# Rotary partner of q and k: from reordered weight copies to permutation matmuls on chip

## The chip, the cores and the metric

The kernel runs on the 8 cores of one Trainium2 chip. Each core takes one of the 8 sequences and runs the same program; nothing passes between the cores. The time is the device time in microseconds of the slowest core, in one launch.

## The reference, cut to what matters

One layer of a streaming encoder over 8192 prompt tokens and 64 sample tokens per core, width 1024: a SwiGLU feed-forward (hidden width 2816) with a LayerNorm, one input projection, sliding-window attention beside a gated recurrence (RG-LRU), an output projection with a LayerNorm, a second feed-forward with a LayerNorm, and a gated embedding. What the change touches is the rotation of q and k behind the input projection:

```python
z = h @ w_in            # [q 512 | k 128 | v 128 | x_lru 512 | gate_lru 512]
def _rope(x, pos):      # x: heads of 64; only the first 16 of each head turn
    x1, x2 = x[..., :8], x[..., 8:16]
    return concat([x1*cos - x2*sin, x2*cos + x1*sin, x[..., 16:]])
q = _rope(q, pos); k = _rope(k, pos)
```

So every turned element needs itself times cos plus its partner (eight columns away in its head) times plus or minus sin.

## The kernel before

**Tiles.** The prompt is cut into 16 tiles of 512 tokens and one last tile of 64 sample tokens, worked one after the other by `tile_prog`. A tile has four subtiles of 128 tokens. `hbuf` holds them token by token in f32; `to_feature_major_s` (lines 655 to 667) turns a subtile with TensorE transposes (L359) into `actT` (bf16, features on the partitions), which ScalarE (q=0) and VectorE (q=1) copy out of PSUM.

**Weights.** No weight stays on the chip. They stream through a ring of `NS` = 6 slots of 1 MB, block by block (`BLOCKS`, lines 159 to 183), 48 blocks to a tile: 11 `up` blocks, 6 `dn` blocks (two halves `hf`, three parts `g` each), 6 `in` blocks (in0 the columns of q, in1 those columns once more with the partners exchanged, in2 the k columns in four versions: plain, partners exchanged, heads exchanged, both; in3 the recurrence, in4 the gate, in5 v), 4 output blocks (`oa`, `ol`), 17 for the second feed-forward, 4 at the end. `w_acquire` names the slot, `w_release` frees it and calls `w_pump` (line 548), which issues the load of the block six places on (an `up` block of both weights is one block). The ring loads are on the SP queue (SyncE), in block order, and SP waits at each until its slot is free.

**Preparation.** The weights arrive in f32 with another layout. In the first tile only, `w_pump` calls `prep_block` (lines 408 to 485) ahead of each block's first load: DMAs on the POOL queue (GpSimd) that cast to bf16 and write `wstream` in device memory. The SP queue waits for a block's preparation before it loads it. These DMAs stand in POOL's program order among its other work, so what stands behind them on POOL (its part of `layer_norm`) is issued after them. Most blocks are 1 to 3 DMAs. in1 is 24 and in2 is 96 (lines 440 to 463), because the exchange of 8 columns by 8 is done by small DMAs, for each of the 8 slices of 128 rows. in0, in1 and in2 are pumped when the three `dn` blocks of half 0 are released, in3, in4 and in5 when those of half 1 are.

**The first feed-forward's end.** In half 1, as each subtile s is done, VectorE adds it to `hbuf`, TensorE turns subtile s-2, and `layer_norm(s)` follows: VectorE (statistics, `nb`), POOL (`rstd`), ScalarE (scale and shift), VectorE (times gamma), POOL (plus beta, 128x1024, L370 `hbuf<-hbuf,bbc`). The turns of subtiles 2 and 3 are left in `pending_T`, for `flush_T`.

**Input projection, where the change is (lines 717 to 762).** Tokens 0 to 255 are worked first, then `flush_T`, then tokens 256 to 511. For each half and each of four 128-column chunks `qc` of q, `inproj_chunk` runs 8 matmuls (256 tokens wide) from in0 into one PSUM bank and 8 from in1 into another. VectorE multiplies the first by `rope_c` into `ftA` and the second by `rope_s` into `ftB`; POOL adds them into `qT`. `ftA` and `ftB` have two buffers each. Then k: two variants (`var`), each two chunks of 8 matmuls of 512 tokens from in2, two multiplications and one POOL add into `kT`. Then v: 32 matmuls of 128 columns from in5, copied by ScalarE. Then the mixed stage, in which steps of attention and of the recurrence alternate; its first matmuls (`attn_A(0)`) read `qT` and `kT`.

**Order and waits.** Every engine runs its instructions in program order. `Prog` turns named reads and writes into semaphore waits. Banks go round eight (`bank`).

**Setup.** SP loads constants. POOL clears `wbd_f`, SP loads 16 small blocks of the recurrence's weights into it, POOL casts it to `wbd`, and then POOL's first preparation DMA is issued.

Of the kernel before, what the change touches and what calls it, by code (L numbers as in the profile page):

```python
# [28 lines left out]
NBLK = 48  # L29
# [129 lines left out]
def block_table():  # L159
# [9 lines left out]
    for i in range(6):  # L169
        blocks.append(("in", i))  # L170
# [19 lines left out]
def blk_extent(b):  # L190
# [6 lines left out]
    if k == "in":  # L197
        return (128, 4096) if b[1] < 5 else (128, 1024)
# [11 lines left out]
def build(ntiles_prompt=SEQ // TILE, with_sample=True):  # L210
# [36 lines left out]
    ident_d = din("ident", [128, 128])  # L247

# [35 lines left out]
    ident = sb("ident_sb", [128, 128])  # L284
    ones_b = sb("ones_b", [128, 64], BF16)
# [8 lines left out]
    wbd_f = sb("wbd_f", [128, 2, 4, 128])  # L294
# [113 lines left out]
    def prep_block(bi):  # L408
# [17 lines left out]
        elif k == "in":  # L426
            j = b[1]
            src = win_d.rearrange("(k p) c -> p k c", p=128)
            if j < 5:
                o4 = dst.rearrange("p (k c) -> p k c", k=8)  # L430
# [6 lines left out]
            elif j == 5:  # L437
                o = dst[:, 0:1024].rearrange("p (k c) -> p k c", k=8)
                prep(o, src[:, :, 640:768])
            elif j == 1:  # L440
                for kk in range(8):
                    o5 = o4[:, kk, :].rearrange("p (h d) -> p h d", h=8)
                    s5 = src[:, kk, 0:512].rearrange("p (h d) -> p h d", h=8)
                    prep(o5[:, :, 16:64], s5[:, :, 16:64])
                    prep(o5[:, :, 0:8], s5[:, :, 8:16])
                    prep(o5[:, :, 8:16], s5[:, :, 0:8])
            elif j == 2:
                for kk in range(8):
                    kcols = src[:, kk, 512:640]
                    prep(o4[:, kk, 0:128], kcols)  # L450
                    o5 = o4[:, kk, 128:256].rearrange("p (h d) -> p h d", h=2)
                    s5 = kcols.rearrange("p (h d) -> p h d", h=2)
                    prep(o5[:, :, 16:64], s5[:, :, 16:64])
                    prep(o5[:, :, 0:8], s5[:, :, 8:16])
                    prep(o5[:, :, 8:16], s5[:, :, 0:8])
                    prep(o4[:, kk, 256:320], kcols[:, 64:128])
                    prep(o4[:, kk, 320:384], kcols[:, 0:64])
                    for hh in range(2):
                        od = o4[:, kk, 384 + hh * 64:384 + (hh + 1) * 64]
                        sd = kcols[:, (1 - hh) * 64:(2 - hh) * 64]  # L460
                        prep(od[:, 16:64], sd[:, 16:64])
                        prep(od[:, 0:8], sd[:, 8:16])
                        prep(od[:, 8:16], sd[:, 0:8])
# [31 lines left out]
    sdma(ident[:], ident_d)  # L495
    for i in range(3):
# [8 lines left out]
    mset("pool", wbd_f[:], 0.0, ("wbdf_ms",))  # L505
    P.final_sems.add("setup2")
    wn = 0
    for ax, src in enumerate((wa_d, wx_d)):
        for cc in range(4):
            for hh in range(2):  # L510
                wn += 1
                o_ = dma("sp", wbd_f[hh * 64:(hh + 1) * 64, ax, cc, hh * 64:(hh + 1) * 64], src[cc * 2 + hh],
                         ("wbdf_ms",), ("wbdf_%d" % wn,), "setup2", nonc=True)
                P.last_w["wbdf"] = o_
    cp("pool", wbd[:], wbd_f[:], ("wbdf", "wbdf_ms"), ("consts2",))
# [157 lines left out]
    def tile_prog(ti, seq, tok0, T, pos0, first, last, nxt=None, preloaded=False):  # L673
# [43 lines left out]
        def inproj_chunk(blk, ci, t0=0, t1=None):  # L717
# [4 lines left out]
            for k in range(8):  # L722
                mm(psum[bk][:, 0:t1 - t0], rg[:, k * 512 + ci * 128:k * 512 + (ci + 1) * 128], actT[:, k, t0:t1],
# [4 lines left out]
        ri = 0  # L728
        for hi_, (t0, t1) in enumerate(halves):
            if hi_ == len(halves) - 1:  # L730
                flush_T()
            W_ = t1 - t0
            for qc in range(4):
                bq = inproj_chunk(0, qc, t0, t1)
                bs = inproj_chunk(1, qc, t0, t1)
                fa, fb = ftA[ri % 2], ftB[ri % 2]
# [380 lines left out]
```

How the kernel before makes its waits and increments, by code:

```python
            def body(eng):  # L134
                for o in prog.streams[engname]:
                    for key, d, fin in o.waits:
                        if key[0] == "d":
                            v = prog.dma_cnt[d.dsem] if fin else d.dval
                            eng.wait_ge(dsems[d.dsem], v)
                        else:
                            eng.wait_ge(esem[d.eng], d.cnt)
                    ins = o.fn(eng)
                    if o.dsem is not None:
                        ins.then_inc(dsems[o.dsem], 16)
                    elif o.signal:
                        ins.then_inc(esem[engname], 1)
                if engname == "sp":
                    for k, v in prog.dma_cnt.items():
                        eng.wait_ge(dsems[k], v)
```

## Time and profile before

| | us |
|---|---|
| median of 2 runs | 7746.52 |
| the two runs | 7599.89 and 7893.15 |
| the profiled execution's own time | 7616.16 |
| its span, slowest core (core 3) | 7614.6 |
| its fastest core (core 0) | 7536.8 |
| TensorE busy | 6090.4 (80%) |
| VectorE, ScalarE, GpSimd busy | 3036.2, 1632.1, 1044.4 |

The span runs from the first to the last instruction. The busy time of TensorE counts matmuls that are waiting in its pipeline, so 80% is not 80% of its peak. "Granted clock" is the share of TensorE's full clock (2.4 GHz) that it was given; its lower level is one half (1.2 GHz). All times in the rows are of core 3.

### The profile page before, as it was taken

The page shows a single profiled execution, that of the slowest core. Times are in us where ns is not written, and L with a number is a line of the kernel's source. Part 1 is how long each engine was busy: PE and PEld are TensorE (multiplying, and loading weights), DVE is VectorE, ACT ScalarE, POOL GpSimd, SP SyncE. Part 2 cuts the span into 40 slices and gives each one's busy share as a digit, 9 for nine tenths or more (in the row PEclk, how much of TensorE's full clock was granted, in tenths as well). Part 3 has the DMA queues.
Part 4 walks back from the last instruction along what each step waited for, and adds up shares of the span by engine and source line. Part 5 has one row for each costly group of instructions (what it writes and reads, how often), then busy time and mean ns, then how long its engine had stood idle before and what let it go on. Part 6 is the DMA issues. An engine that isn't in the chain of part 4 may idle for free.

```text
span 7614.6 us, 100795 instructions; the slowest of 8 cores (7536.8 to 7614.6 us)
## 1 busy us (share of the span) xinstructions
PE 6090.4 (80%) x33302; PEld 3325.1 (44%) x33302; DVE 3036.2 (40%) x5649; ACT 1632.1 (21%) x3079; POOL 1044.4 (14%) x1329
## 2 busy tenths in 40 slices
PE   4226698888888898888888888888888888888884
PEld 2113254444444454444444444444454454444442
DVE  1013244343434444443434434443444444353432
ACT  0012122131312122131312112131212113131211
POOL 1132011110201111110201110110201111010110
PEclk9657798989898998989898998989898898989886
DMA  9997823424242332424242332424232342424336
GB/s 159 75 59 104 172 96 112 144 93 143 74 155 77 136 126 107 150 84 152 74 151 80 129 133 102 154 78 154 78 140 91 116 146 95 150 84 149 82 134 200
DMA packets 272280, 901.92 MB, mean 118 GB/s; under 512 B 72896, under 2 KB 145920, under 8 KB 191264
## 3 DMA queue, kind: packets, MB, share of 16 engines
q1 hardware_dynamic: 154864, 818.91, 31.5%
q0 software_dynamic: 116912, 76.56, 19.9%
q8 instruction: 282, 4.62, 0.3%
q14 instruction: 222, 1.82, 0.1%
HBM read 906.19 MB, written 78.92 MB: 129 GB/s over the span
## 4 chain that ended last, share of the span: by engine, by line
PE 56%; issue 13%; DVE 10%; ACT 8%; DMA 6%; POOL 4%; another core or an unknown queue 2%; SPq 0%; DVEq 0%; ACTq 0%; POOLq 0%
PE ps_all L356 54%; DVE stats L640 3%; ACT hbuf L367 2%; DMA hbuf<-x 2%; DVE hbuf L378 2%; PE ps_all L359 2%; DVE L_xc L378 1%; DMA ring<-wstream 1%; POOL wstream L400 1%; POOL rstd L370 1%; DMA y<-hbuf 1%; ACT LS L367 1%; ACT PT L367 1%; ACT LA L367 1%
## 5 line engine op out<-in xcount | busy, mean ns | idle before, releaser
L356 PE MATMUL ps_all<-actT,ring 128*128 128x512 bf16 (+2 forms) x18784 | 3301.1, 340 | 276.5 <-DMA ring<-wstream 122.6
L356 PEld LDWEIGHTS ps_all<-actT,ring 128*128 128x128 bf16 x18784 | 1839.9, 103 | 1655.5 <-issue 451.1
L356 PE MATMUL ps_all<-ring,hid 128*128 128x512 bf16 (+1 forms) x5720 | 1270.9, 384 | 118.1 <-DMA ring<-wstream 117.4
L378 DVE SCALAR_TENSOR_TENSOR ftB<-ftA,ps_all 128x512 f32<-128x512 f32 (+2 forms) x1070 | 612.3, 572 | 1569.3 <-ACT ftA L367 1471.7
L367 ACT ACTIVATE ftA<-ps_all 128x512 f32<-128x512 f32 (+2 forms) x1070 | 539.3, 505 | 2355.9 <-PE ps_all L356 2012.7
L356 PEld LDWEIGHTS ps_all<-ring,hid 128*128 128x128 bf16 (+1 forms) x5720 | 564.7, 99 | 806.0 <-issue 155.0
L359 PE MATMUL ps_all<-ident_sb,hbuf 128*128 128x128 f32 (+1 forms) x2080 | 310.8, 306 | 569.4 <-POOL hbuf L370 274.9
L367 ACT ACTIVATE hbuf<-hbuf,nb,rstd 128x1024 f32<-128x1024 f32 (+1 forms) x195 | 241.8, 1240 | 2278.0 <-DVE nb L378 2278.0
L378 DVE SCALAR_TENSOR_TENSOR hbuf<-hbuf,ps_all 128x512 f32<-128x512 f32 (+1 forms) x390 | 267.0, 685 | 929.6 <-PE ps_all L356 929.6
L370 DVE TENSOR_TENSOR hid<-ftB,ps_all 128x512 bf16<-128x512 f32 (+2 forms) x940 | 523.7, 557 | 175.6 <-PE ps_all L356 102.8
L374 POOL TENSOR_SCALAR rstd<-mv 128x1 f32<-128x1 f32 (+1 forms) x195 | 43.2, 222 | 3766.4 <-DVE mv L642 3766.3
L359 PEld LDWEIGHTS ps_all<-ident_sb,hbuf 128*128 128x128 f32 (+1 forms) x2080 | 269.1, 160 | 635.3 <-issue 634.3
L370 POOL TENSOR_TENSOR hbuf<-hbuf,bbc 128x1024 f32<-128x1024 f32 (+1 forms) x195 | 458.5, 2351 | 612.6 <-DVE hbuf L370 605.8
L356 PE MATMUL ps_all<-Vb,PT 128*64 128x65 bf16 (+1 forms) x2048 | 373.2, 244 | 122.3 <-ACT PT L367 89.2
L356 PEld LDWEIGHTS ps_all<-Vb,PT 128*64 128x64 bf16 (+1 forms) x2048 | 242.3, 119 | 270.4 <-issue 163.2
L370 DVE TENSOR_TENSOR hbuf<-hbuf,gbc 128x1024 f32<-128x1024 f32 (+1 forms) x195 | 238.8, 1225 | 293.5 <-ACT hbuf L367 293.5
L356 PE MATMUL ps_all<-ring,actT 128*128 128x512 bf16 (+2 forms) x1560 | 309.0, 350 | 29.9 <-DMA ring<-wstream 26.9
L640 DVE BATCH_NORM_STATS2 stats<-hbuf 128x6 f32<-128x512 f32 (+1 forms) x390 | 269.5, 691 | 31.4 <-DVE stats L640 0.9
L383 DVE CAST actT<-ps_all 128x512 bf16<-128x512 f32 x260 | 175.2, 682 | 258.0 <-PE ps_all L359 255.7
L382 ACT CAST actT<-ps_all 128x512 bf16<-128x512 f32 x260 | 149.4, 575 | 389.4 <-PE ps_all L359 389.3
L356 PEld LDWEIGHTS ps_all<-ring,actT 128*128 128x128 bf16 (+1 forms) x1560 | 140.7, 104 | 171.2 <-issue 69.4
L367 ACT ACTIVATE PT<-ps_all 64x256 bf16<-64x256 f32 (+1 forms) x512 | 194.6, 380 | 43.0 <-PE ps_all L356 16.3
(94 smaller groups left out, 3159.9 us busy)
## 6 DMA issues: line engine op xcount, KB each, us to landing
ring<-wstream SPq DMA_DIRECT2D x629, 1024.0 KB, 5.9
ring<-wstream SPq DMA_DIRECT2D x68, 768.0 KB
ring<-wstream SPq DMA_DIRECT2D x68, 512.0 KB, 4.6
y<-hbuf SPq DMA_DIRECT2D x64, 512.0 KB, 5.2
hbuf<-x POOLq DMA_DIRECT2D x60, 512.0 KB, 10.4
ring<-wstream SPq DMA_DIRECT2D x51, 256.0 KB, 3.0
wstream<-ffn_wg POOLq DMA_DIRECT2D x22, 512.0 KB, 48.8
wstream<-ffn_wu POOLq DMA_DIRECT2D x22, 512.0 KB, 58.5
```

The lines of the kernel that those rows point to most:

```text
L356: return P.op("pe", lambda e: e.matmul(out, lhsT, rhs, start=start, stop=stop), reads, writes)
L359: return P.op("pe", lambda e: e.transpose(out, in_, idn), reads, writes)
L367: return P.op("act", lambda e: e.activation(out, in_, func, **kw), reads, writes)
L370: return P.op(eng, lambda e: e.tensor_tensor(out, a, b, op), reads, writes)
L374: return P.op(eng, lambda e: e.tensor_scalar(out, a, s1, None, op0), reads, writes)
L378: return P.op("dve", lambda e: e.scalar_tensor_tensor(out, a, s, b, op0, op1), reads, writes)
L382: return P.op("act", lambda e: e.copy(out, in_), reads, writes)
L383: return P.op(eng, lambda e: e.tensor_copy(out, in_), reads, writes)
L400: return e.dma_start(out=out, in_=in_)
L640: P.op("dve", lambda e, c=c: e.bn_stats(stats[0:nt, c, :], hv[0:nt, c * 512:(c + 1) * 512]), (hn,), (sn,))
```

## The change

It drops block in1 and three of the four versions in block in2: 47 blocks to a tile, in2 is 256 KB instead of 1 MB. The partner values come from a matmul with a constant 0/1 matrix: ScalarE copies the q chunk out of PSUM into a bf16 buffer `qb`, and one matmul with `perm[:, 0, :]` as weights gives its rows exchanged. Each q item is finished one item late (`pend`), so that the next chunk's 8 matmuls stand between the copy and the permutation. For k there is one chunk of 8 matmuls, one copy and three permutation matmuls (partners, heads, both); nothing stands between copy and permutations. In setup the three matrices are loaded by SP and cast by VectorE, and `wbd` is built in two passes through `ftB`, one after the other.

```diff
-    for i in range(6):
+    for i in (0, 2, 3, 4, 5):
         blocks.append(("in", i))
...
-            elif j == 1:
-                for kk in range(8):
-                    o5 = o4[:, kk, :].rearrange("p (h d) -> p h d", h=8)
-                    s5 = src[:, kk, 0:512].rearrange("p (h d) -> p h d", h=8)
-                    prep(o5[:, :, 16:64], s5[:, :, 16:64])
-                    prep(o5[:, :, 0:8], s5[:, :, 8:16])
-                    prep(o5[:, :, 8:16], s5[:, :, 0:8])
             elif j == 2:
-                for kk in range(8):
-                    kcols = src[:, kk, 512:640]
-                    prep(o4[:, kk, 0:128], kcols)
...
+                o = dst[:, 0:1024].rearrange("p (k c) -> p k c", k=8)
+                prep(o, src[:, :, 512:640])
...
+    perm_f = ftA[0][:, 0:384].rearrange("p (a b) -> p a b", a=3)
+    dma("sp", perm_f, perm_d, (), ("ftA0",), "permld")
+    cp("dve", perm[:], perm_f, ("ftA0",), ("consts2",))
...
-    mset("pool", wbd_f[:], 0.0, ("wbdf_ms",))
     for ax, src in enumerate((wa_d, wx_d)):
+        stage = ftB[ax][:, :].rearrange("p (c d) -> p c d", c=4)
+        mset("pool", ftB[ax][:, :], 0.0, ("ftB%d" % ax,))
         for cc in range(4):
             for hh in range(2):
...
+        cp("pool", wbd[:, ax, :, :], stage, ("wbdf%d" % ax, "ftB%d" % ax), ("consts2", "ftB%d" % ax))
-    cp("pool", wbd[:], wbd_f[:], ("wbdf", "wbdf_ms"), ("consts2",))
...
+        items = [(hi_, t0, t1, qc) for hi_, (t0, t1) in enumerate(halves) for qc in range(4)]
+        pend = []
+        def q_finish(it, bq, ri):
+            hi_, t0, t1, qc = it
+            W_ = t1 - t0
+            bs = bank()
+            mm(psum[bs][:, 0:W_], perm[:, 0, :], qb[ri % 2][:, 0:W_], True, True, ("qb%d" % (ri % 2),) + CONST,
+               ("ps%d" % bs,))
+            fa, fb = ftA[ri % 2], ftB[ri % 2]
+            tt("dve", fa[:, 0:W_], psum[bq][:, 0:W_], rope_c[:, t0:t1], ALU.mult,
+               ("ps%d" % bq, "rope"), ("ftA%d" % (ri % 2),))
+            tt("dve", fb[:, 0:W_], psum[bs][:, 0:W_], rope_s[:, t0:t1], ALU.mult,
+               ("ps%d" % bs, "rope"), ("ftB%d" % (ri % 2),))
+            tt("pool", qT[:, qc, t0:t1], fa[:, 0:W_], fb[:, 0:W_], ALU.add,
+               ("ftA%d" % (ri % 2), "ftB%d" % (ri % 2)), ("qT",))
+        for ri, it in enumerate(items):
+            hi_, t0, t1, qc = it
+            if hi_ == len(halves) - 1 and qc == 0:
+                flush_T()
+            bq = inproj_chunk(0, qc, t0, t1)
+            cp("act", qb[ri % 2][:, 0:t1 - t0], psum[bq][:, 0:t1 - t0], ("ps%d" % bq,), ("qb%d" % (ri % 2),))
+            if pend:
+                q_finish(*pend.pop())
+            pend.append((it, bq, ri))
+        q_finish(*pend.pop())
...
-        for var in range(2):
-            bq = inproj_chunk(2, var * 2)
-            bs = inproj_chunk(2, var * 2 + 1)
+        bkk = inproj_chunk(2, 0)
+        cp("act", qb[0][:, 0:T], psum[bkk][:, 0:T], ("ps%d" % bkk,), ("qb0",))
+        bks, bkd, bkds = bank(), bank(), bank()
+        for pi_, bb in ((0, bks), (1, bkd), (2, bkds)):
+            mm(psum[bb][:, 0:T], perm[:, pi_, :], qb[0][:, 0:T], True, True, ("qb0",) + CONST, ("ps%d" % bb,))
+        for var, (bq, bs) in enumerate(((bkk, bks), (bkd, bkds))):
```

## Rows read from the trace of the kernel before

**Rows 1.** Cores: span and mean granted clock of the slowest.

```profile
core 3: 7614.6 us, clock 0.859
```

**Rows 2.** Waits, 0 to 960 us: engine, line, releaser; total us, times, longest.

```profile
PE ps_all L356 <- DMA ring<-wstream: 259.0, 33, 48.7
PE ps_all L359 <- POOL hbuf L370: 152.9, 2, 149.0
```

**Rows 3.** Timeline of TensorE in the first tile: start, length, ..., idle before.

```profile
263.79 3.57 PE L356 MATMUL ps_all<-ring,hid 128*128 128x512 bf16 x8 [11.16 <-DMA ring<-wstream]
316.06 12.28 PE L356 MATMUL ps_all<-ring,hid 128*128 128x512 bf16 x50 [48.70 <-DMA ring<-wstream]
477.34 1.94 PE L359 MATMUL ps_all<-ident_sb,hbuf 128*128 128x128 f32 x8 [149.00 <-POOL hbuf L370]
...
547.67 3.46 PE L356 MATMUL ps_all<-ring,actT 128*128 128x128 bf16 x32 [26.94 <-DMA ring<-wstream]
```

**Rows 4.** Timeline of GpSimd in the first tile.

```profile
348.90 28.99 POOL L400 DMA_DIRECT2D wstream<-w_in  x47 [72.65 <-issue]
...
495.71 2.36 POOL L370 TENSOR_TENSOR hbuf<-hbuf,bbc 128x1024 f32<-128x1024 f32 x1 [3.13 <-DVE hbuf L370]
498.01 2.63 POOL L400 DMA_DIRECT2D wstream<-w_in  x3
```

**Rows 5.** Busy time by stretch: PE, PEld, DVE, ACT, POOL, granted clock, DMA share, GB/s.

```profile
200.00:250.00 50.00, 31.16 (x115) 12.20 (x114) 4.81 (x7) 1.19 (x2) 2.02 (x3) 0.80 1.02 158
...
350.00:400.00 50.00, 0.00 (x0) 0.00 (x0) 0.00 (x0) 0.00 (x0) 27.89 (x46) 0.50 7.24 9
```

**Rows 6.** DMA packets from 330 to 480 us.

```profile
DMA packets 28160, 3.60 MB, mean 24 GB/s; under 512 B 27904, under 2 KB 27904, under 8 KB 27904
```

**Rows 7.** DMA issues, whole span: out<-in, queue, count, KB each, us to landing.

```profile
wstream<-w_in POOLq DMA_DIRECT2D x32, 2.0 KB, 24.7
```

**Rows 8.** Ring loads issued on SP from 240 to 255 and from 255 to 270 us.

```profile
L352 SPq DMA_DIRECT2D ring<-wstream x1: 319/319/319, 249.6 to 249.6; - x1
L352 SPq DMA_DIRECT2D ring<-wstream x1: 320/320/320, 261.6 to 261.6; - x1
```

**Rows 9.** Timeline of TensorE in the second tile, around the input projection.

```profile
1072.86 8.48 PE L356 MATMUL ps_all<-actT,ring 128*128 128x256 bf16 x60 [0.94 <-DVE actT L383]
1081.18 1.91 PE L359 MATMUL ps_all<-ident_sb,hbuf 128*128 128x128 f32 x16
...
1084.82 13.62 PE L356 MATMUL ps_all<-actT,ring 128*128 128x256 bf16 x92 [0.64 <-DVE actT L383]
...
1101.02 0.51 PE L356 MATMUL ps_all<-qT,kT 64*128 64x128 bf16 x4 [0.80 <-POOL kT L370]
```

**Rows 10.** Timeline of GpSimd and of ScalarE there: the last LayerNorm.

```profile
1078.71 2.35 POOL L370 TENSOR_TENSOR hbuf<-hbuf,bbc 128x1024 f32<-128x1024 f32 x1 [3.12 <-DVE hbuf L370]
1076.00 1.24 ACT L367 ACTIVATE hbuf<-hbuf,nb,rstd 128x1024 f32<-128x1024 f32 x1 [5.33 <-DVE nb L378]
```

**Rows 11.** Groups by form: busy us, mean ns.

```profile
L382 ACT CAST actT<-ps_all 128x512 bf16<-128x512 f32 x256 | 147.9, 578 | 375.2 <-PE ps_all L359 375.2
...
L370 DVE TENSOR_TENSOR ftA<-ps_all,rope_c 128x256 f32<-128x256 f32 x128 | 54.0, 422 | 78.7 <-PE ps_all L356 42.1 <-POOL qT L370 34.4 <-DVE ftB L370 0.3
...
L382 ACT CAST pT<-ps_all 128x256 bf16<-128x256 f32 x64 | 23.5, 368 | 4.4 <-ACT pT L382 0.4
```

**Rows 12.** Timeline of the setup: SP's last 8 small loads, POOL's first preparation.

```profile
21.08 4.95 SPq L349 DMA_DIRECT2D wbd_f<-lru_wx  x8
...
29.65 1.14 POOL L400 DMA_DIRECT2D wstream<-ffn_wg  x1 [0.40 <-issue]
```

**Rows 13.** Busy time by stretch in the second tile, columns as in rows 5.

```profile
1070.00:1080.00 10.00, 8.15 (x54) 6.19 (x55) 6.63 (x12) 1.90 (x3) 4.43 (x4) 0.67 0.19 78
...
1140.00:1160.00 20.00, 15.27 (x91) 8.29 (x89) 10.93 (x28) 12.21 (x26) 1.61 (x4) 0.67 0.09 27
```

More of the change, by code:

```diff
@@ L28 @@
 SLOT = 4096
-NBLK = 48
+NBLK = 47
 HEAD_PERM = [0, 2, 1, 3, 4, 6, 5, 7]
@@ L247, in build @@
     ident_d = din("ident", [128, 128])
+    perm_d = din("perm", [128, 3, 128])
     y_d = dout("y", [NTOK, D])
@@ L284, in build @@
     ident = sb("ident_sb", [128, 128])
+    perm = sb("perm_b", [128, 3, 128], BF16)
+    qb = [sb("qb%d" % i, [128, TILE], BF16) for i in range(2)]
     ones_b = sb("ones_b", [128, 64], BF16)
@@ L727, in tile_prog @@
         halves = ((0, 256), (256, 512)) if T == TILE else ((0, T),)
-        ri = 0
-        for hi_, (t0, t1) in enumerate(halves):
-            if hi_ == len(halves) - 1:
-                flush_T()
[L732 to L736, printed above, removed]
-                tt("dve", fa[:, 0:W_], psum[bq][:, 0:W_], rope_c[:, t0:t1], ALU.mult,
-                   ("ps%d" % bq, "rope"), ("ftA%d" % (ri % 2),))
-                tt("dve", fb[:, 0:W_], psum[bs][:, 0:W_], rope_s[:, t0:t1], ALU.mult,
-                   ("ps%d" % bs, "rope"), ("ftB%d" % (ri % 2),))
-                tt("pool", qT[:, qc, t0:t1], fa[:, 0:W_], fb[:, 0:W_], ALU.add,
-                   ("ftA%d" % (ri % 2), "ftB%d" % (ri % 2)), ("qT",))
-                ri += 1
+        items = [(hi_, t0, t1, qc) for hi_, (t0, t1) in enumerate(halves) for qc in range(4)]
@@ L1066, in rope_tables, with perm_tables, partner @@
     return tab
+def perm_tables():
+    pm = np.zeros((128, 3, 128), np.float32)
+    def partner(d):
+        dd = d % 64
+        if dd < 8:
+            return d + 8
+        if dd < 16:
+            return d - 8
+        return None
+    for m in range(128):
+        p_ = partner(m)
+        if p_ is not None:
+            pm[p_, 0, m] = 1.0
+        sw = (m + 64) % 128
+        pm[sw, 1, m] = 1.0
+        p2 = partner(sw)
+        if p2 is not None:
+            pm[p2, 2, m] = 1.0
+    return pm
 _CACHE = {}
@@ L1084 @@
     ident = np.eye(128, dtype=np.float32)
+    perm = perm_tables()
     shared = {
@@ L1092 @@
         "lru_wx": f(lru_wx[0]), "lru_bx": f(lru_bx[0]), "lru_lambda": f(lru_lambda[0]),
-        "rope": rope, "ident": ident,
+        "rope": rope, "ident": ident, "perm": perm,
     }
```

30 lines of the change are left out of this document (8 added, 22 removed).

## The prediction

> **What bounds the kernel now.** I read the cores first: the slowest took 7614.6 us [rows 1]; its own time is 7616.16 us, 1.6 us more, and I count against that. It lies 1.7% below the median of the two runs and close to the lower one. Next come TensorE's longest waits in the first tile. It waited 259.0 us for ring loads and 152.9 us for one LayerNorm, 149.0 us of that in one piece [rows 2]. The timeline puts both in the first feed-forward's end [rows 3]. TensorE runs 8 matmuls at 263.79, then waits 48.70 us for the last `dn` load, runs 50 matmuls, and stands 149.00 us before the turn of subtile 0. The reader is to see what was late on the other side of each wait.
>
> On GpSimd the LayerNorm of subtile 0 stands behind the preparation of in1 and in2. POOL had waited 72.65 us when, at 348.90, it issued 47 small DMAs, and a second batch like it followed [rows 4]. In this time the DMA engines carried almost nothing: 158 GB/s at 200 to 250 us, 9 GB/s at 350 to 400, at a DMA share of 7.24, the sum of packets that overlap and all take long [rows 5]. Of 28,160 packets between 330 and 480 us, 27,904 were under 512 B [rows 6], from DMAs as small as 2 KB [rows 7]. The ring load of the last `dn` block was issued at 261.6 and its matmuls began at 316.06, 54.5 us later; the one before, issued at 249.6, began at 263.79, 14.2 us later [rows 3, 8]. So about 120 DMAs hold up both a ring load and a LayerNorm. That happens once, whatever the number of tiles.
>
> From the second tile on the input projection is bound otherwise. TensorE's first q half, 60 of its 64 matmuls in 8.48 us, and the turns of subtiles 2 and 3 at 1081.18 [rows 9] end where the last LayerNorm's POOL add ends, 1078.71 + 2.35 = 1081.06 [rows 10]. The second half, k and v run without a gap: 92 matmuls in 13.62 us. Attention then starts at 1101.02, with 0.80 us of waiting for `kT` [rows 9]. That stretch is TensorE's own.
>
> **Part 1: the small preparation goes (first tile).** 120 DMAs become one. The POOL queue then has in0, in2 and in3 ahead of the LayerNorm, all issued while other preparation drains. The last `dn` load would land 14.2 us after issue, at 275.8 instead of 316.06: 40.3 us. The 149.0 us wait goes except for the LayerNorm itself, which overlaps the 12.28 us of 50 matmuls; I leave 1 us of it, bounds 0 and 5: 148.0 us. Sum 188.3 us.
>
> What is late next: v. Its load waited for the preparation of in3, in4, in5, issued at 498.01 as the LayerNorm of subtile 3 ended [rows 4]; v began at 547.67, 49.7 us later, after 26.94 us of waiting [rows 3]. Now in3 is prepared earlier, one place ahead in the ring. Two preparations landed 12.0 us apart at 768 KB [rows 8], so 1 MB is 12 to 16 us; I take 14. v starts 14 us sooner against that LayerNorm. POOL issues eight `oa` DMAs ahead of the first q add in exchange (some 0.6 us each by the 28.99 us for 47 [rows 4], so 5 us), but v waits anyway: nothing. The q and k savings of this one tile are swallowed by the same wait. Sum for the first tile 188.3 + 14 = 202.
>
> in2 is still written in rows of 256 B, 1024 of them. 28,160 packets took these 150 us [rows 6], so 1024 take 5.5 us at the same rate; bounds 0 and 16 (as a 1 MB block). It is behind the `dn` blocks and TensorE wants it only for k, some 30 us later: nothing, up to 5.
>
> The Trainium skill bears on that (DMA: Bandwidth & Descriptors, Specifications): below 512 B a transfer becomes read-modify-write, so by it in2 stays on the slow side. The collapse to 9 GB/s with nearly all packets under 512 B agrees with it [rows 5, 6]. By the rule in2 costs as much per row as in1 did, and the sum would be up to 5 us less; by the wait for v, nothing.
>
> **Part 2: the matmuls (15 prompt tiles).** Per column the stretch of 92 matmuls gives 13.62 us / (60 x 256 + 32 x 512 = 31,744 columns) = 0.43 ns [rows 9].
> - First q half: half its matmuls go (32 x 256 columns, 3.5 us). But the turn of subtile 3 waits for the LayerNorm's add at 1081.06, which doesn't move. Also, the copies into `qb` stand on ScalarE behind the LayerNorm's activation, which ends at 1077.24 [rows 10], so the first permutation waits until about 1077.7, with chunks 2 and 3 queued behind it on TensorE. 0.9 + 0.9 us of chunks and three permutations fit before 1081. What is gained: VectorE's copies out of the turns come after three items instead of four, two operations of 0.42 us [rows 11]: 0.8 us.
> - Second q half and k: 64 x 256 + 32 x 512 = 32,768 columns become 32 x 256 + 8 x 512, plus 5 x 256 + 3 x 512 of permutations = 15,104. 17,664 x 0.43 = 7.6 us saved.
> - New waits: the last q permutation waits for its copy. A ScalarE copy of this size took 368 ns, one of 512 columns 578 ns [rows 11]; with 0.2 us of handing over, 0.6 us, and 0.8 us for k. Behind them stand TensorE's k chunk and v. The other copies are covered by the next chunk (8 x 256 columns, 0.9 us). VectorE needs 2 x 0.42 us to an item, under TensorE's 0.97: no new bound, but a thin one.
> - The k adds: `kT` is ready when two POOL adds are done, and v covers less of them; the wait of 0.80 us grows by some 0.6.
>
> Sum 7.6 + 0.8 - 0.6 - 0.8 - 0.6 = 6.4 us to a tile; 15 tiles: 96 us. Bounds: nothing (rival B) to the full column saving of both halves, 64 x 256 + 24 x 512 less 8 x 256 + 3 x 512 = 25,088 columns, 10.8 us; so 0 to 162 us in all.
>
> **Part 3: small ones.** Ring traffic falls by 1.75 MB a tile, but no wait of TensorE in the later tiles lies at in1 or in2: nothing. The sample tile has an eighth of the tokens: 6.4 / 8 = 0.8 us. Setup: the second eight small loads (4.95 us) now wait until the first eight landed and POOL has cast and cleared. That puts landing, cast and clearing, some 4 us, and the issue of `perm`'s load, 0.4 us, ahead of POOL's first preparation at 29.65 [rows 12]. All that follows in the first tile is paced by preparation, so it is paid: 4.4 us, bounds 0 and 8.
>
> **Sum.** 7616.2 - 202 - 96 - 0.8 + 4.4 = 7321.8: 7322 us, 3.9% less.
>
> **The rivals.**
> - B, the matmuls bring nothing. While TensorE waits for ScalarE in the first q half, its clock stays at the lower level: 0.67 was the mean at 1070 to 1080 [rows 13], and with still more holes there the rise comes later. If the second half and k run at 1.2 GHz, their 15,104 columns cost 6.5 us more, just what was gained. For it: three new places where TensorE stands. Against: from 1085 on work is dense. 7322 + 96 = 7418.
> - C, half of the first tile's stall stays: in0, in2 and in3 are now prepared in the same stretch, and ring loads share the DMA engines with them. For it: loads took up to 54.5 us there. Against: the load beside ordinary preparation took 14.2. 7322 + 100 = 7422.
> - D, TensorE saves in full, because the LayerNorm's end is no wall: 15 x (10.8 - 6.4) = 66 us more, 7256. Against: the first half ends within 0.2 us of that LayerNorm [rows 9, 10].
> - E, slower than before. The q, k and v stretch, broken by handovers, leaves TensorE on its lower level, and it enters the mixed stage so and stays. There 15.27 of 20 us are busy at a mean clock of 0.67 [rows 13]; at 0.5 the same work is 20.5 us, 5.2 more for each 20 us. For 80 us of mixed stage that is 21 us, with the 6.5 us of B 27, less the 6.4 gained: 21 us a tile, 315 us in all, 7616 - 202 + 315 = 7729. It decides from 14 us lost to a tile. Against: the stage has its own holes already and its clock is set by them.
> - F, the small DMAs' time was not the cause and the wait stays (the change doesn't do what it says): 7616 - 96 = 7520.
>
> The Trainium skill speaks for B and E (TensorE: Matmul & The Clock Gate, HAM oscillation): waits between bursts put the engine back on its half clock, and the warm-up is paid anew in each. No row here shows it for holes of 0.6 us.
>
> **How the numbers follow.** Forecast 0.56, B 0.17, C 0.11, D 0.09, E 0.03, F 0.04. A measurement tells about 2% from no change. The range goes from D's side, 7250, to beyond B and C, 7440. Faster by over 2% means below 7464: the forecast, B, C, D, in all 0.92 after leaving 0.01 of C out; within 2%: F and that 0.01, 0.05; slower 0.03.
>
> **What would show it.** Right: no TensorE wait over 30 us between 250 and 500 us; the turn of subtile 0 near 293 us (with the setup's 4.4); v near 350; the first tile some 200 us shorter; from `flush_T` to attention 6 us less a tile, and the turns of subtile 3 still ending with the POOL add. Wrong: a wait of 100 us left in front of a LayerNorm (F, C), a granted clock near 0.5 to 0.7 after `flush_T` (B), or in the mixed stage (E).

## The result, and the profile after

| us | before | after |
|---|---|---|
| median of the launches (10 and 11) | 7853.21 | 7405.99 |
| shortest launch | 7599.04 | 7317.11 |
| profiled execution, its own time | 7616.16 | 7366.27 |
| mean span of its 8 cores | 7577.5 | 7304.1 |

The ratio is 0.9638, 95% interval 0.9621 to 0.9655: 3.6% less time. The medians contain launches in which the cores of one die (four neighbouring cores) had a lower clock and took longer; the ratio leaves these out, and without them the launches took 7599 to 7600 us before and 7317 to 7334 us after, two of them 7322.

The rows of some cores in the profiled execution of after: cores 0 and 1 are the longest and have the lowest mean clock.

```profile
core 0: 7363.4 us, clock 0.854
core 1: 7336.4 us, clock 0.855
...
core 3: 7290.4 us, clock 0.856
...
core 5: 7277.0 us, clock 0.865
```

I read the first tile on core 3, as before, and the steady tiles on core 5. First the page's counts of after. Before, the page had 72,896 packets under 512 B of 272,280, and q0, the queue of the preparation, had 116,912 packets and 19.9% of the engines; TensorE was busy 6090.4 us.

```profile
PE 5961.4 (81%) x31588; PEld 3223.9 (44%) x32021; DVE 3033.0 (41%) x5650; ACT 1686.1 (23%) x3228; POOL 970.3 (13%) x1212
...
DMA packets 229152, 868.93 MB, mean 118 GB/s; under 512 B 31824, under 2 KB 104976, under 8 KB 152496
...
q0 software_dynamic: 76096, 74.72, 6.8%
```

TensorE's timeline in the first tile, core 3, answers to [rows 3]:

```profile
234.70 3.57 PE L358 MATMUL ps_all<-ring,hid 128*128 128x512 bf16 x8 [8.15 <-DMA ring<-wstream]
...
278.61 15.47 PE L358 MATMUL ps_all<-ring,hid 128*128 128x512 bf16 x50 [6.13 <-DMA ring<-wstream]
293.91 1.23 PE L361 MATMUL ps_all<-ident_sb,hbuf 128*128 128x128 f32 x8
...
338.81 3.57 PE L358 MATMUL ps_all<-ring,actT 128*128 128x128 bf16 x32 [7.37 <-DMA ring<-wstream]
```

The 48.70 us wait is 6.13, the 149.00 us wait is gone, and v waits 7.37 us instead of 26.94. GpSimd's timeline, answering to [rows 4], shows the other side. Its last preparation before the LayerNorms is one DMA at 156.00; then it waits 127.39 us for VectorE's statistics, so it is early instead of late. The LayerNorm of subtile 3 ends at 311.55 instead of 498.07, and the preparations of in4 and in5 follow as before:

```profile
156.00 0.83 POOL L402 DMA_DIRECT2D wstream<-w_in  x1 [14.48 <-issue]
284.21 0.23 POOL L376 TENSOR_SCALAR rstd<-mv 128x1 f32<-128x1 f32 x1 [127.39 <-DVE mv L627]
...
309.21 2.34 POOL L372 TENSOR_TENSOR hbuf<-hbuf,bbc 128x1024 f32<-128x1024 f32 x1 [3.13 <-DVE hbuf L372]
311.50 1.75 POOL L402 DMA_DIRECT2D wstream<-w_in  x2
```

Busy time of core 3 by stretch (columns of [rows 5]) and its packets from 330 to 480 us, against [rows 5, 6]. TensorE, which was idle from 350 to 400, is busy 38 of 50 us; the packets fell from 28,160 to 12,569, those under 512 B from 27,904 to 472.

```profile
200.00:250.00 50.00, 26.99 (x82) 9.52 (x81) 4.81 (x7) 1.79 (x3) 0.00 (x0) 0.64 1.03 159
350.00:400.00 50.00, 38.00 (x196) 18.89 (x195) 27.18 (x65) 28.96 (x63) 4.63 (x11) 0.56 0.00 0
```
```profile
DMA packets 12569, 12.81 MB, mean 85 GB/s; under 512 B 472, under 2 KB 11445, under 8 KB 12085
```

The steady tiles next: TensorE's timeline on core 5 in the second tile, against [rows 9].

```profile
838.73 2.72 PE L358 MATMUL ps_all<-actT,ring 128*128 128x256 bf16 x12 [1.36 <-DVE actT L385]
...
843.51 0.37 PE L358 MATMUL ps_all<-qb,perm_b 128*128 128x256 bf16 x1 [2.06 <-ACT qb L384]
...
847.51 1.96 PE L361 MATMUL ps_all<-ident_sb,hbuf 128*128 128x128 f32 x16
849.96 1.05 PE L358 MATMUL ps_all<-actT,ring 128*128 128x256 bf16 x8 [0.49 <-ACT actT L384]
...
854.73 0.27 PE L358 MATMUL ps_all<-qb,perm_b 128*128 128x256 bf16 x1 [0.67 <-DVE ftA L372]
...
858.01 0.81 PE L358 MATMUL ps_all<-qb,perm_b 128*128 128x512 bf16 x3 [1.26 <-ACT qb L384]
858.65 1.95 PE L358 MATMUL ps_all<-ring,actT 128*128 128x128 bf16 x32
862.45 0.51 PE L358 MATMUL ps_all<-qT,kT 64*128 64x128 bf16 x4 [1.85 <-POOL kT L372]
```

The waits that the prediction added are all here: 2.06 us before the first permutation (with the chunks behind it), 0.67 before the last one of q, 1.26 before the three of k, and 1.85 instead of 0.80 before attention. The turns at 847.51 still begin just behind the last LayerNorm's POOL add, which ends at 844.58 + 2.35 = 846.93 (against [rows 10]):

```profile
844.58 2.35 POOL L372 TENSOR_TENSOR hbuf<-hbuf,bbc 128x1024 f32<-128x1024 f32 x1 [3.12 <-DVE hbuf L372]
```

From there to attention it is 862.45 - 846.93 = 15.52 us; the same distance in [rows 9, 10] is 1101.02 - 1081.06 = 19.96. Over all 8 cores and the 14 tiles between the first mark and the last (explained below), 112 distances, the means are 15.16 and 20.13: 4.97 us less. The clock (columns of [rows 5]) is full behind `flush_T`:

```profile
830.00:850.00 20.00, 12.54 (x70) 8.29 (x69) 11.81 (x23) 5.40 (x9) 10.77 (x10) 0.74 0.25 92
850.00:870.00 20.00, 15.01 (x118) 9.18 (x118) 9.52 (x19) 5.60 (x15) 6.35 (x8) 1.00 0.17 54
```

This is not one lucky tile. In the 8 us that begin 3 us behind that add, the mean granted clock is 1.00 in 110 of the 112 tiles of after and in 107 of the 112 of before.

**A mark in each tile.** To take the time apart I use POOL's copy `kT<-kT`, which ends the mixed stage of each of the first 15 tiles. Its group gives the first and the last start. Here are core 3 of before and core 3 of after; the columns behind the count are shortest, median and longest ns, then first and last start.

```profile
L383 POOL COPY kT<-kT x15: 399/399/412, 629.3 to 6774.7; 128x256 bf16<-128x256 bf16 x15
```
```profile
L385 POOL COPY kT<-kT x15: 399/399/736, 419.7 to 6463.7; 128x256 bf16<-128x256 bf16 x15
```

Between the two starts lie 14 tiles. The table has means over the 8 cores of each profiled execution; the last column is the time from the last mark to the end.

| us | first mark | per tile | tail |
|---|---|---|---|
| before | 614.6 | 437.63 | 836.2 |
| after | 416.5 | 431.83 | 842.0 |

So 198.1 us came out of the first tile at once, and 5.8 us out of each later one. How exact is that? The kernels that keep the 120 small DMAs (before, and runs 2, 6 and 7 below) have first marks of 599.6 to 614.6, so the mark of before is good to some 15 us. Those with the later tiles of after (runs 2, 3 and 4) need 431.4 to 432.4 us a tile, so the 5.8 is good to some 0.6. By the stretches of a tile, before and after: from the mark to the last LayerNorm's add 343.46 and 342.75, from there to attention 20.13 and 15.16, from there to the next mark 74.04 and 73.92. The change's own stretch gives 5.0 of the 5.8; in run 2, with the same matmuls, the other two stretches give 0.2. (The tail of after has cores 0 and 1 in it, whose clock was the lowest; run 2 below, with the same matmuls, has 828.4.)

### The profile page after: what moved, and what is told of

It reads as the page before. It is cut to its first block, busy times and chain, and to the rows that moved or that the text cites. A ratio compares the mean times of both kernels' runs of the same rounds, so it can differ in the third digit from the quotient of the medians.

```text
span 7363.4 us, 98138 instructions; the slowest of 8 cores (7277.0 to 7363.4 us)
## 1 busy us (share of the span) xinstructions
PE 5961.4 (81%) x31588; PEld 3223.9 (44%) x32021; DVE 3033.0 (41%) x5650; ACT 1686.1 (23%) x3228; POOL 970.3 (13%) x1212
## 4 chain that ended last, share of the span: by engine, by line
PE 56%; DVE 10%; issue 10%; ACT 9%; DMA 6%; another core or an unknown queue 4%; POOL 3%; SPq 1%; DVEq 0%; ACTq 0%; POOLq 0%
PE ps_all L358 54%; DVE stats L625 3%; ACT hbuf L369 2%; PE ps_all L361 2%; DMA hbuf<-x 2%; DVE hbuf L380 2%; DVE L_xc L380 1%; POOL rstd L372 1%; DMA y<-hbuf 1%; DMA wstream<-ffn_wu 1%; DMA ring<-wstream 1%; ACT LS L369 1%; ACT PT L369 1%; ACT LA L369 1%
## 5 line engine op out<-in xcount | busy, mean ns | idle before, releaser
L358 PE MATMUL ps_all<-actT,ring 128*128 128x512 bf16 (+2 forms) x17048 | 3123.3, 345 | 289.2 <-DMA ring<-wstream 110.5
L358 PEld LDWEIGHTS ps_all<-actT,ring 128*128 128x128 bf16 x17320 | 1706.0, 103 | 1609.9 <-issue 521.5
L358 PE MATMUL ps_all<-ring,hid 128*128 128x512 bf16 (+1 forms) x5624 | 1290.5, 389 | 71.8 <-DMA ring<-wstream 65.2
L358 PE MATMUL ps_all<-ring,actT 128*128 128x512 bf16 (+2 forms) x1528 | 310.4, 354 | 13.8 <-DMA ring<-wstream 11.8
```

The costliest lines, as they stand in the source:

```text
L358: return P.op("pe", lambda e: e.matmul(out, lhsT, rhs, start=start, stop=stop), reads, writes)
```

## The experiments

My theory: the small preparation DMAs are worth 188 us in the first tile, mostly as a stall of GpSimd's program order, and the matmuls are worth 6.4 us a tile, in the second half of q and in k. The rivals are those of the prediction, and one more: that the number of DMAs counts rather than their rows.

**1. Before, with in1 and in2 prepared in one large DMA each.** The matmuls stay as they were; partners and exchanged versions of k are not in the weights, so q and k are not rotated as in the reference.

```diff
-            elif j == 1:
-                for kk in range(8):
...
-            elif j == 2:
-                for kk in range(8):
...
+            elif j in (1, 2):
+                prep(o4, src[:, :, 0:512])
```

> The kernel before, with one thing changed: in1 and in2 are each prepared by a single DMA in rows of 1 KB, the plain q columns, instead of 24 and 96 small ones. So the partner and head-exchanged values are left out (the rotation multiplies other numbers), all matmuls, ring loads and copies stay. My theory (the small rows of the preparation cost the first tile about 188 us of waiting, the matmuls are a matter of their own): 7600 goes to about 7410, a ratio of 0.975 (0.972 to 0.979), and v's wait in the first tile stays over 20 us. Rival (what helps is that a block and its bytes are gone, so this edit, which keeps both blocks, gains little): 0.99 or more.

First mark 434.3, 437.09 a tile: 180.3 us gained in the first tile, 0.5 in each of the others. Shortest launch 7417.39; ratio 0.9784 [0.9651, 0.9918]. That interval reaches the rival's 0.99; the mark does not. Core 3, TensorE's wait between 200 and 600 us, and then its timeline:

```profile
PE ps_all L359 <- POOL hbuf L370: 4.9, 1, 4.9
```
```profile
275.26 13.79 PE L356 MATMUL ps_all<-ring,hid 128*128 128x512 bf16 x50 [6.21 <-DMA ring<-wstream]
...
352.09 3.57 PE L356 MATMUL ps_all<-ring,actT 128*128 128x128 bf16 x32 [22.16 <-DMA ring<-wstream]
```

The first part of the gain comes with the 120 small DMAs alone. v still waits 22.16 us here, 14.8 more than after. On the mean of the cores v begins 45.2 us behind the LayerNorm of subtile 3, as before (45.3), and 28.6 in after. The forecast put this on in3's place in the ring, "v starts 14 us sooner"; the size fits, the reason was not tested by itself.

**2. After, with the 120 small DMAs put back.** They fill memory `xs_d` that nobody reads, ahead of in2's preparation; the matmuls are those of after.

```diff
             elif j == 2:
+                o4 = xs_d[0].rearrange("p (k c) -> p k c", k=8)
+                for kk in range(8):
+                    o5 = o4[:, kk, :].rearrange("p (h d) -> p h d", h=8)
+                    s5 = src[:, kk, 0:512].rearrange("p (h d) -> p h d", h=8)
+                    prep(o5[:, :, 16:64], s5[:, :, 16:64])
...
                 o = dst[:, 0:1024].rearrange("p (k c) -> p k c", k=8)
```

> The changed kernel, with the 120 small preparation DMAs of before put back in the same place of GpSimd's order, into spare device memory that nothing reads. It has the new matmuls, copies and ring blocks, and the old preparation. Theory (two parts that add up): only the later tiles' part is left, 15 times 5.8 us or 87, less 4 to 7 us of the longer setup: about 7520, a ratio of 0.989 (0.986 to 0.992). Rival (the small DMAs are hidden and the gain comes from the matmuls): 0.964, as the changed kernel.

First mark 611.3, 432.40 a tile; launches 7522.3 and 7526.81, as expected. The first tile is as long as before, the later ones 5.2 us shorter; in the whole mean span 7577.5 - 7493.3 = 84.2 us, where the prediction had 96.8 for this part. In core 3's waits the stall is back:

```profile
PE ps_all L362 <- POOL hbuf L373: 165.2, 1, 165.2
```

By the marks, run 1 takes 180.3 us out of the first tile and run 2 takes 3.3, the change 198.1; 14.5 are left. They are no bigger than the uncertainty of the mark of before. v's earlier place is not absent from run 2: v begins 34.6 us behind the LayerNorm, 10.7 sooner than before, but that LayerNorm ended 7.3 us later, some 2.5 of them the longer setup. After and run 1, neither of which has the small rows, lie 17.8 us apart. A later tile gives 0.5 and 5.2, the change 5.8.

**3. After, with 120 DMAs more, but in rows of 1 KB.** Each writes 8 partitions by 512 columns into unread memory.

```diff
+                for n_ in range(120):
+                    kk, r_ = n_ % 8, n_ // 8 * 8
+                    xo = xs_d[0].rearrange("p (k c) -> p k c", k=8)[r_:r_ + 8, kk, :]
+                    prep(xo, src[r_:r_ + 8, kk, 0:512])
```

> The changed kernel plus 120 small DMAs at the same place, each of only 8 rows of 1 KB into spare device memory: the count of before with 960 rows instead of some 40,000. If the rows are what costs, the time stays within 10 us of the changed kernel: ratio to before 0.963 to 0.966 (issuing them takes GpSimd some 75 us, of the 127 us in which it waits for the first LayerNorm there). If the number of DMAs is what costs (their issue, their fixed time, their places in the queue), 100 to 200 us come back: 0.977 to 0.990.

First mark 425.1, 8.6 us later than after; shortest launch 7323.78, ratio 0.9631 [0.9603, 0.9659]. TensorE's wait for the LayerNorm on core 3 is 6.0 us. The number of DMAs by itself is not what stalls.

**4. After, with 5 DMAs more, in 40,960 rows of 16 B.**

```diff
+                for n_ in range(5):
+                    xo = xs_d[0].rearrange("p (c e) -> p c e", e=64)[:, :, n_ * 8:n_ * 8 + 8]
+                    xi = src[:, n_, 0:512].rearrange("p (c d) -> p c d", d=8)
+                    prep(xo, xi)
```

> The changed kernel plus 5 DMAs at the same place, each of 8192 rows of 16 B written into spare device memory: the rows of before (41,000) in 5 DMAs. If the rows cost, at the rate of before (28,160 packets in 150 us), 41,000 take 218 us and most of it, 100 to 200 us, is waited for: ratio to before 0.977 to 0.990. If the number of DMAs costs, nothing comes back: 0.964.

First mark 534.0 (526.3 to 541.5 over the cores), 117.5 us later than after; shortest launch 7434.07. Core 3: TensorE's wait for the LayerNorm, and the DMA traffic from 280 to 380 us.

```profile
394.85 1.94 PE L362 MATMUL ps_all<-ident_sb,hbuf 128*128 128x128 f32 x8 [93.29 <-POOL hbuf L373]
```
```profile
DMA packets 30760, 1.63 MB, mean 16 GB/s; under 512 B 30593, under 2 KB 30621, under 8 KB 30632
```

GpSimd's timeline on core 3 shows how five DMAs stop a LayerNorm: the engine stands some 24 us ahead of each of the last three issues, and the LayerNorm's first step comes right behind the last. That it waits there for the DMA before to drain is my reading; 24.1 + 2.7 us for 8192 rows, 3.3 for 1000, fits the price below.

```profile
330.43 2.71 POOL L403 DMA_DIRECT2D wspare<-w_in  x1 [24.42 <-issue]
...
383.70 2.71 POOL L403 DMA_DIRECT2D wspare<-w_in  x1 [24.10 <-issue]
...
388.22 0.23 POOL L377 TENSOR_SCALAR rstd<-mv 128x1 f32<-128x1 f32 x1
```

How much of the 188 us would go if the small DMAs stayed and only stood behind the LayerNorm was not tried.

Five DMAs with as many rows do much of what 120 did: 117.5 us, 2.9 for 1000 rows. But not all of it. Run 2 came 194.8 us later than after with about the same number of small packets, and the expectation, at the rate of before, had 218 us for this run. The preparation queue in the pages of run 2 and of this run (packets, MB, share of 16 engines; 6.8% in after):

```profile
q0 software_dynamic: 117952, 76.83, 21.4%
```
```profile
q0 software_dynamic: 117136, 75.38, 10.1%
```

So a row of before, 16 to 256 B long, cost more than one of these, by 77 us in all, and run 3's 8.6 us for the number of DMAs doesn't cover that. Whether the rows' length, their place or the mixture makes the rest is open. If in2's 1024 rows of 256 B cost as little as these, they are worth about 3 us in after; at run 2's 194.8 us for some 41,000 it is 5. Both are estimates.

**5. The same five DMAs, each row in a 512-B line of its own.**

```diff
-    xs_d = nc.dram_tensor("wspare", [2, 128, SLOT], BF16, kind="Internal").ap()
+    xs_d = nc.dram_tensor("wspare", [5, 128, 64 * 256], BF16, kind="Internal").ap()
...
-                    xo = xs_d[0].rearrange("p (c e) -> p c e", e=64)[:, :, n_ * 8:n_ * 8 + 8]
+                    xo = xs_d[n_].rearrange("p (c e) -> p c e", e=256)[:, :, 0:8]
```

> The run with 5 DMAs of 8192 rows of 16 B once more (it cost 112 us against the changed kernel, its first tile's mixed stage ended 117 us later), but each row is written into a 512-byte line of its own instead of eight rows lying in one line. If neighbouring partial writes to one line are what takes the time, the first tile comes back to within 30 us of the changed kernel. If each small row costs the same wherever it lands, the 117 us stay (100 to 135).

First mark 548.3, 131.8 us later than after, from one execution on another chip. I use this mark alone, since the later tiles are those of after. That rows share a line with their neighbours is not what makes them slow; apart they cost no less. The Trainium skill (DMA: Bandwidth & Descriptors, Specifications) says that below 512 B a transfer becomes read-modify-write. Runs 3, 4 and 5 agree that such rows are the slow ones: 8.6 us for 960 rows of 1 KB in 120 DMAs against 117.5 and 131.8 for 40,960 rows of 16 B in five. How the engine handles them inside, no run here shows.

**6 and 7. Before, without the in1 matmuls of one half of q.** The rotation of that half then takes the unexchanged product, a bank that is already there. First the half before `flush_T`, then the half behind it, each 32 matmuls of 256 columns less.

```diff
-                bs = inproj_chunk(1, qc, t0, t1)
+                bs = bq if (len(halves) == 2 and hi_ == 0) else inproj_chunk(1, qc, t0, t1)
```

> The kernel before, without the in1 matmuls of the first half (tokens 0 to 255) in the 16 prompt tiles: 32 matmuls of 256 columns a tile fewer, 0.11 us each by the trace, 3.5 us a tile. The sine product reads the plain chunk there (so half of the rotated q values are other numbers). Theory (this half ends with the last LayerNorm, whoever is fast): at most 0.8 us a tile, 12 us in all, ratio 0.998 to 1.000. Rival (TensorE's work there is the bound): 16 times 3.5 = 56 us, ratio 0.993.

> The same number of in1 matmuls left out, but those of the second half (tokens 256 to 511). Theory (here TensorE is the bound): 15 times 3.5 = 52 us and nothing in the first tile, where v's load is waited for: ratio 0.993 (0.992 to 0.995), about 45 us faster than the kernel that leaves them out in the first half. Rival (both halves alike): the two kernels are within 10 us of each other.

The first half: 437.48 a tile, as before (437.63); launches 7592 to 7605, ratio 0.9942 [0.9858, 1.0026]. This interval holds the rival's 0.993 too, so the marks have to decide, and they leave nothing of its 3.5 us a tile. The shortest launch is 15 us under the 7607 of before on that chip. Against the profile of before, the first mark is 15.0 us earlier, and the turn of subtile 0, which stands ahead of everything that the edit touches, already 11.8: most of that is the first tile's scatter, not the edit.

The second half: launches 7526 to 7551, ratio 0.987 [0.98, 0.9941]; the shortest is 82 us under that 7607. I had expected a difference of 45 between the two runs and see 67. From the last LayerNorm's add to attention, mean of 112 tiles, it is 20.13 us before, 16.78 without the second half, 3.35 less where 8192 x 0.43 ns = 3.5 was expected, and 21.34 without the first: not shorter but longer by 1.2. The whole tile doesn't show this 1.2; the stretches ahead of the add and behind attention were 0.4 and 0.9 shorter there, and I don't know why. The profiled execution without the second half took 7674.46 us, longer than the launches named, so I read only this distance from it. 15 x 3.35 = 50 of the 82 us are explained; where the rest came from I did not follow. Core 5 without the first half: the LayerNorm's add, and TensorE, which now stands 2.84 us before the turn.

```profile
1009.66 2.34 POOL L370 TENSOR_TENSOR hbuf<-hbuf,bbc 128x1024 f32<-128x1024 f32 x1 [3.13 <-DVE hbuf L370]
```
```profile
1012.14 1.06 PE L359 MATMUL ps_all<-ident_sb,hbuf 128*128 128x128 f32 x8 [2.84 <-POOL hbuf L370]
...
1015.75 15.86 PE L356 MATMUL ps_all<-actT,ring 128*128 128x256 bf16 x92 [1.04 <-DVE actT L383]
```

And the clock of the stretch behind it in this tile, 0.79, where before had 1.00 in the same place (second fence, before, core 5):

```profile
1017.00:1025.00 8.00, 8.00 (x58) 6.35 (x57) 3.09 (x8) 0.00 (x0) 2.17 (x3) 0.79 0.02 4
```
```profile
1067.00:1075.00 8.00, 7.86 (x68) 6.60 (x69) 3.84 (x9) 0.00 (x0) 2.33 (x4) 1.00 0.05 11
```

The same 92 matmuls take 15.86 us instead of 13.62 [rows 9]. Over the 112 tiles, in the 8 us that begin 3 us behind the add, the mean granted clock is below 0.9 in 76 without the first half and in 5 before. Where it stayed at 1.00 (36 tiles) the add and attention lie 19.98 us apart, as in such tiles of before (20.06); in the 76 others 21.98. So there are two things. The LayerNorm is the wall: at full clock, 32 matmuls less bring 0.1 us. And holes in front of it can cost clock behind it, which is rival B's mechanism. Not each hole does: TensorE waited 1.3 to 3.3 us before the turn in all 112 tiles, and the 36 that kept the full clock had waits of 1.9 to 2.7, in the middle of that range. In the changed kernel it does not bite: its clock there is 1.00 in 110 of 112 tiles (above).

**8. After, with the handovers covered.** The k chunk and its copy come right behind `flush_T`, the three k permutations behind the next q chunk, and the last q item is finished behind v's first 8 matmuls. The k products get buffers of the recurrence that are free then.

```diff
             if second and qc == 0:
                 flush_T()
+                bkk = inproj_chunk(2, 0)
+                cp("act", LXCB[0][:, 0:T], psum[bkk][:, 0:T], ("ps%d" % bkk,), ("L_xcb0",))
+                if pend:
+                    q_finish(*pend.pop())
             bq = inproj_chunk(0, qc, t0, t1)
+            if second and qc == 0:
+                k_perm(bkk)
...
+            if s == 0:
+                q_finish(*pend.pop())
```

> The changed kernel, reordered: the k chunk comes right behind the turns of subtiles 2 and 3, its three permutations behind the next q chunk, and the last q permutation behind v's first 8 matmuls; the k products use buffers of the recurrence that are free then. Nothing is left out. Theory (the three holes of the changed kernel, about 0.65 us before the last q permutation, 1.0 to 1.3 before k's and 1.3 to 1.9 before attention, are handovers that other matmuls can cover): 2.8 us a tile, 45 us in all, 7322 becomes 7277 or a ratio to before of 0.958. Rival (VectorE and GpSimd set the pace, so the wait only moves): as the changed kernel, 0.964.

430.32 a tile, 1.5 less than after; launches 7291.99 and 7308.12. From the LayerNorm's add to attention it is 13.12 us instead of 15.16, so 2.0 less of the 2.8 expected, and the whole tile shows 1.5 of them. The second half's waits for `qb` and the one for `kT` are gone, but on core 5 attention now waits for the last q add:

```profile
841.80 0.27 PE L358 MATMUL ps_all<-qb,perm_b 128*128 128x256 bf16 x1
...
850.64 0.60 PE L358 MATMUL ps_all<-qT,kT 64*128 64x128 bf16 x4 [1.61 <-POOL qT L372]
```

Half to three quarters of what I expected: part of a handover removed in one place came back in the next.

**9. Run 8, and the first tile's preparations put forward.** The preparations of the first six blocks are issued ahead of the constants' loads, and v's block stands ahead of the recurrence's two.

```diff
-    for i in (0, 2, 3, 4, 5):
+    for i in (0, 2, 5, 3, 4):
...
+    for i_ in range(NS):
+        prep_block(i_)
...
-            if i < NBLK:
+            if NS <= i < NBLK:
```

> The kernel of the run before (k early), and two edits that touch the first tile only: GpSimd issues the preparation of the first six blocks ahead of the setup (before, its first preparation DMA stood at 30 to 35 us behind the loads and casts of the recurrence's weights), and v's block goes ahead of the recurrence's in the block order, so that it is prepared with in0 and in2. Nothing is left out. Theory (the first tile is paced by preparation from its first DMA on): 25 us for the early start and 8 to 12 for v, together about 7243, ratio 0.953. Rival (preparation and the loads of constants and x share the DMA engines, so the early start is given back): 0.957.

First mark 393.2, 430.94 a tile. Median 7271.82, shortest launch 7264.04, ratio to before 0.951 [0.9446, 0.9575]: faster than both kernels. Against run 8 the first mark is 24.6 us earlier, where I had expected 33 to 37. By the means of the cores, against run 8: GpSimd's first preparation is at 1.58 us instead of 34.73, the turn of subtile 0 comes 21.4 us sooner, and v begins 15.7 us behind the LayerNorm instead of 25.1, 9.4 sooner. So each edit seems to have given about its share, though I did not run them apart, and some 6 us were lost again behind v. Of the 33 us of early start 21.4 arrive. SP's rows show one reason: issuing eight small constant loads takes 14.27 us beside the preparation, where it took 4.95 [rows 12].

```profile
1.58 1.14 POOL L402 DMA_DIRECT2D wstream<-ffn_wg  x1 [0.90 <-POOLq L213]
```
```profile
31.30 14.27 SPq L351 DMA_DIRECT2D ftB<-lru_wa  x8
```

**10. Run 9, with the pending q item finished ahead of the k chunk**, so that the last q add should come sooner.

```diff
+                if pend:
+                    q_finish(*pend.pop())
                 bkk = inproj_chunk(2, 0)
                 cp("act", LXCB[0][:, 0:T], psum[bkk][:, 0:T], ("ps%d" % bkk,), ("L_xcb0",))
-                if pend:
-                    q_finish(*pend.pop())
```

> The kernel with k early and preparation ahead of the setup, with the permutation of the fourth q chunk put ahead of the k chunk, so that GpSimd gets its fourth q add about 1.9 us sooner. Nothing is left out. In the run with k early, attention waited 1.6 us for the last q add. Theory (the end of the stage is now GpSimd's and VectorE's queue, which stood idle until 842.9 in that tile): 0.9 us a tile, 14 us in all, 7250 to 7260, ratio 0.952 to 0.955. Rival (the queue is bound by the k products): as the kernel before this, 7265.

430.74 a tile, shortest launch 7264.18, ratio 0.9552 [0.9505, 0.9599]: the same as run 9, a miss of mine and what the rival had said. Attention still waits 1.60 us for `qT` on core 5, and GpSimd's k add stands before it, itself 2.10 us late for VectorE's product:

```profile
835.53 1.27 POOL L372 TENSOR_TENSOR kT<-L_g 128x512 bf16<-128x512 f32 x1 [2.10 <-DVE L_g L372]
```
```profile
841.98 0.51 PE L358 MATMUL ps_all<-qT,kT 64*128 64x128 bf16 x4 [1.60 <-POOL qT L372]
```

Which of VectorE's operations would have to move is open; I did not try it.

## Why the prediction was right and where it was wrong

**The failed step: the base.** The forecast subtracts from the profiled execution, "its own time is 7616.16 us, 1.6 us more, and I count against that", and of the median of the two runs, 7746.52, it says only that its base "lies 1.7% below". The range was built on 7616.16 alone. The measured ratio on the shown median is 0.9638 x 7746.52 = 7466 us, beyond my upper end of 7440; on the profiled time it is 0.9638 x 7616.16 = 7340 us, 18 from the forecast. The two runs shown were 7599.89 and 7893.15: the median of two so far apart is a time at which no execution ran. The gain as a share is what carries over: forecast 294.3 / 7616.2 = 3.9%, measured 3.6%. The upper end needed to allow for a base 1.7% higher. That two launches of after took 7322 us, the forecast to the microsecond, is luck: the base of 7616 was 16 us above the 7600 of such launches before, and the gain between those launches, 278 us, was 16 less than the 294 forecast.

**The first tile: confirmed, "Sum for the first tile 188.3 + 14 = 202", with the setup 197.6.** Measured by the first mark: 198.1, good to some 15. That the two differ by only 0.5 is chance. Its parts: the turn of subtile 0 moved from 468.2 to 288.1 on the mean of the cores, 180.1 us, where 188.3 - 4.4 = 183.9 were forecast (on core 3 it came at 293.91, forecast "near 293"). What is behind it gained 18.0 instead of 14: v began 28.6 us after the LayerNorm of subtile 3 instead of 45.3 on the mean of the cores. The 14 us came from "Two preparations landed 12.0 us apart"; the rows behind it are the issue times of two ring loads, of which only the second is of 768 KB, so the term was an estimate with a weaker ground than it says. Run 1 gives the first part alone, 180.3; run 2 takes it back. The load of the last `dn` block came as forecast: its matmuls at 278.61, forecast 275.8 + 4.4 = 280.2.

**The tile: "Sum 7.6 + 0.8 - 0.6 - 0.8 - 0.6 = 6.4 us" was too much by 0.6 to 1.4.** After has 5.8 a tile less, run 2 5.2, and the stretch from the LayerNorm's add to attention, for which the sum was made, 4.97. The shape was right: runs 6 and 7 show the wall in the first half and the gain in the second. Too small were the handovers. In the waits of TensorE over the later tiles of core 5, first before, then after:

```profile
PE ps_all L356 <- POOL kT L370: 11.4, 14, 1.0
```
```profile
PE ps_all L358 <- ACT qb L384: 46.9, 31, 2.3
...
PE ps_all L358 <- POOL kT L372: 27.1, 15, 2.1
PE ps_all L358 <- DVE ftB L372: 8.6, 13, 0.7
```

The wait for `kT` is 27.1 / 15 = 1.8 instead of 0.8 us, so it grew by 1.0 where I had 0.6. The 46.9 us for `qb` are mostly the 2.06 of the first half, which the LayerNorm hides, and the 1.26 for k, where I had 0.8. The last q item's, 8.6 / 13 = 0.66, was right. I had taken 578 ns for the copy [rows 11] and 0.2 us for handing over, once. ScalarE's row for the k copy shows two handovers: the k chunk ended at 858.01 - 1.26 = 856.75, the copy began 0.42 us later, and the permutations began 0.25 us after its end.

```profile
857.17 0.59 ACT L384 CAST qb<-ps_all 128x512 bf16<-128x512 f32 x1 [2.69 <-PE ps_all L358]
```

With these terms the sum is 7.6 + 0.8 - 0.66 - 1.26 - 1.0 = 5.5, still 0.5 above the 4.97. The other 0.8 us a tile of the 5.8 lie outside the stretch; run 2, with the same matmuls, has 0.2 there, so I take most of them for scatter.

**Setup: 4.4 forecast, 2.75 measured.** GpSimd's first preparation is at 31.69 on the mean of the cores before and 34.44 after.

**The rivals.** B falls: full clock behind `flush_T` in 110 of 112 tiles. Its mechanism exists, as run 6 shows, but hardly in the changed kernel. The Trainium skill (TensorE: Matmul & The Clock Gate, HAM oscillation) tells of waits between bursts that put the engine back on its half clock. Run 6 agrees in 76 of its 112 tiles, with 0.79 in the one shown; the changed kernel, with waits of 0.67 and 1.26 us in the stretch from 850 to 870, shows 1.00. C falls: no TensorE wait over 11.1 us for a ring load from 200 to 600 us on core 3. D falls by run 6. E falls with B: tiles got shorter. F falls by runs 1 and 2. Of its own signs, "no TensorE wait over 30 us", "near 293 us" (293.91) and the turns still ending with the POOL add came true; v came 11 us earlier than the "near 350" (338.81), and "from `flush_T` to attention 6 us less a tile" is 5.0.

## What to carry to other kernels

A rearrangement of a weight in device memory by small rows is paid for by others: the load that was on its way then (54.5 us instead of 14.2) and the compute that stands behind the issues on the same engine (a LayerNorm, 149 us). Few long rows cost little, however many DMAs carry them (run 3); many short ones cost much in five DMAs too (run 4). It is cheap to make the partner on TensorE from data already there, if each copy out of PSUM has independent matmuls behind it and the last one does too. Before counting matmuls that go, ask what ends the stretch that they are in: the same 32 matmuls were worth nothing on one side of a LayerNorm and 3.35 us a tile on the other. When a gain of some microseconds is read from a mark, first ask how far the mark moves between kernels that are alike up to it; here 15 us. And a forecast in microseconds stands on a base: where two shown runs lie 4% apart, the range has to include what that does to the number.

## What the runs showed of the hardware that I had not expected

- 40,960 rows of 16 B in a converting copy within device memory made the first tile 117.5 us longer packed side by side and 131.8 us longer 512 B apart (2.9 and 3.2 us for 1000); 960 rows of 1 KB in 120 DMAs made it 8.6 us longer; about as many rows as the 40,960, of 16 to 256 B in 120 DMAs, 194.8 us.
- Issuing eight small loads on SP took 4.95 us in the setup of before and 14.27 us beside large preparations.
- A handover from TensorE over a ScalarE copy of 128x512 back to TensorE left TensorE waiting 1.26 us, twice the copy's own 0.59.
- With TensorE waiting 1.3 to 3.3 us in front of dense work in every tile, the next stretch had a granted clock below 0.9 in 76 of 112 tiles and 1.00 in 36. The lower clock made the way to attention 2.0 us longer, 21.98 instead of 19.98.
